# Weight-sum sets, operand splits and one low part at other places in a hand-scheduled retention and attention kernel

## The reference

```python
def retention_layer(x, w_in, w_out, pos):
    h = x @ w_in                                    # 1024 -> 6144
    q, k, v, g = jnp.split(h, [D_MODEL, 2 * D_MODEL, 2 * D_MODEL + RET_WIDTH], axis=-1)
    q = rope(q.reshape(bsz, s, RET_HEADS, RET_QK_DIM), pos)
    k = rope(k.reshape(bsz, s, RET_HEADS, RET_QK_DIM), pos) * RET_QK_DIM ** -0.5
...
    att = jnp.einsum('bhncd,bhnmd->bhncm', qc, kc) * dec[None, :, None]
    inner = jnp.einsum('bhncm,bhnme->bhnce', att, vc)
...
        cross = jnp.einsum('bhcd,bhde->bhce', qn, state) * xi
        state = state * g_chunk + jnp.einsum('bhcd,bhce->bhde', kn * zeta, vn)
...
    return (jax.nn.silu(g) * r) @ w_out             # 2048 -> 1024

def swa_layer(x, w_in, w_out, sinks, k_band, v_band, bias, key_valid):
    q, gate = jnp.split(x @ w_in, 2, axis=-1)
    sc = jnp.einsum('bncvgd,bnkvd->bvgnck', q, k_band) + bias
...
    m = jnp.maximum(sc.max(-1, keepdims=True), sink)
    p = jnp.exp(sc - m)
    p = p / (p.sum(-1, keepdims=True) + jnp.exp(sink - m))
    o = jnp.einsum('bvgnck,bnkvd->bncvgd', p, v_band)
    return (o * jax.nn.silu(gate)) @ w_out
```

## Time and profile before

| | |
|---|---|
| median of 3 runs | 2386.39 us |
| the three runs | 2385.63, 2386.39, 2390.29 us |
| the profiled execution | 2392.8 us |
| its span in the trace | 2391.0 us |
| PE busy | 2324.5 us, 97% |
| DVE busy | 1776.2 us, 74% |
| ACT busy | 1180.2 us, 49% |
| POOL busy | 329.6 us, 14% |
| DMA, mean over the span | 183 GB/s, 437.10 MB |

### The profile page before, as it was taken

The page is one execution under the profiler, slowest core; times in us unless marked ns, Lnnn a source line. Parts: engine busy times, 40 slices in busy tenths (PEclk is TensorE's granted clock), DMA queues, the critical chain, the costliest instruction groups (busy, mean ns, idle before and its releaser), DMA issues.

```text
span 2391.0 us, 31112 instructions
## 1 busy us (share of the span) xinstructions
PE 2324.5 (97%) x11554; PEld 1898.8 (79%) x11554; DVE 1776.2 (74%) x2575; ACT 1180.2 (49%) x1757; POOL 329.6 (14%) x346
## 2 busy tenths in 40 slices
PE   8999999999999999999999999999999999999996
PEld 6878878877788888887788888888777888888775
DVE  7778798856857669885696866886488668788458
ACT  4344455357435445535754545553665445453463
POOL 1212211112000111111201001110110110011032
PEclk9999999999999999999999999999999999999998
DMA  8776668643725445864384454575257344454323
GB/s 306 260 274 244 232 220 295 227 160 119 260 96 164 153 128 172 288 223 155 118 286 132 164 167 132 172 269 177 71 174 261 128 132 159 132 199 145 117 79 123
DMA packets 211798, 437.10 MB, mean 183 GB/s; under 512 B 14848, under 2 KB 52240, under 8 KB 208064
## 3 DMA queue, kind: packets, MB, share of 16 engines
q1 hardware_dynamic: 197568, 369.28, 46.6%
q0 software_dynamic: 14080, 65.83, 7.6%
HBM read 373.45 MB, written 57.41 MB: 180 GB/s over the span
## 4 chain that ended last, share of the span: by engine, by line
PE 76%; DVE 11%; DMA 5%; issue 4%; ACT 2%; SPq 1%; POOL 0%; DVEq 0%; ACTq 0%; POOLq 0%
PE accs L693 21%; PE accs L694 20%; PE accs L695 20%; DVE w_lo L1396 3%; PE bank L693 3%; PE bank L695 3%; PE bank L694 3%; DMA stage<-t_prep 2%; PE bank L959 2%; DMA stage<-ret_w_in 2%; PE bank L968 1%; PE bank L978 1%; PE bank L799 1%; ACT w_hi L1044 1%; DVE z L1721 1%
## 5 line engine op out<-in xcount | busy, mean ns | idle before, releaser
L1396 DVE TENSOR_TENSOR w_lo<-stage,w_hi 128x1024 fp32r<-128x1024 f32 x524 | 650.7, 1248 | 372.8 <-ACT w_hi L1044 371.3
L1044 ACT ACTIVATE w_hi<-stage 128x1024 fp32r<-128x1024 f32 x524 | 550.8, 1056 | 499.7 <-PE accs L695 184.7
L693 PE MATMUL accs<-w_hi,xs 128*128 128x512 f32 x1136 | 451.4, 397 | 12.2 <-DVE w_lo L1396 4.8
L695 PE MATMUL accs<-w_hi,xs 128*128 128x512 f32 x1136 | 444.2, 391 | 0.0
L694 PE MATMUL accs<-w_lo,xs 128*128 128x512 f32 x1136 | 443.9, 391 | 0.0
L693 PEld LDWEIGHTS accs<-w_hi,xs 128*128 128x128 f32 x1136 | 214.4, 189 | 61.1 <-issue 10.8
L695 PEld LDWEIGHTS accs<-w_hi,xs 128*128 128x128 f32 x1136 | 214.1, 188 | 45.8
L693 PE MATMUL accs<-x_hi,w_hi 128*128 128x512 f32 (+1 forms) x640 | 247.4, 387 | 2.7 <-DVE qT L1958 1.4
L694 PEld LDWEIGHTS accs<-w_lo,xs 128*128 128x128 f32 x1136 | 214.6, 189 | 42.5
L694 PE MATMUL accs<-x_lo,w_hi 128*128 128x512 f32 (+1 forms) x640 | 238.8, 373 | 0.0
L695 PE MATMUL accs<-x_hi,w_lo 128*128 128x512 f32 (+1 forms) x640 | 237.1, 371 | 0.0
(11 more groups left out here) (205 smaller groups left out, 3805.3 us busy)
## 6 DMA issues: line engine op xcount, KB each, us to landing
stage<-t_prep SPq DMA_DIRECT2D x208, 512.0 KB, 4.4
stage<-ret_w_in SPq DMA_DIRECT2D x100, 512.0 KB, 3.9
stage<-ret_w_in SPq DMA_DIRECT2D x128, 256.0 KB, 2.9
stage<-swa_w_in SPq DMA_DIRECT2D x64, 512.0 KB, 4.1
t_prep<-t_buf POOLq DMA_DIRECT2D x28, 1024.0 KB, 5.9
stage<-ret_w_out SPq DMA_DIRECT2D x48, 512.0 KB, 3.7
cs<-rope_t SPq DMA_DIRECT2D x16, 1024.0 KB, 7.1
t_buf<-ret_w_in POOLq DMA_DIRECT2D x32, 512.0 KB, 9.1
```

The costliest lines, as they stand in the source:

```text
L693: mm(dst, lhs[0], rhs[0], start=start, stop=False, skip_group_check=reopened)
L695: return mm(dst, lhs[1], rhs[0], start=False, stop=stop, skip_group_check=reopened)
L1044: copy(w_hi[:, RING[g] % HS], stage[:, RING[g] % LS], ACT.Copy).then_inc(w_hi_made, 1)
L1396: nc.vector.tensor_tensor(w_lo[:, RING[g] % LS], stage[:, RING[g] % LS], w_hi[:, RING[g] % HS].bitcast(F32), sub).then_inc(w_split, 1)
```

## The change

Five edits, four of them to tables of slots.

- Set 16 is loaded in slot 30 of block 0 (it was 23).
- Set 23 is loaded, made and stored one slot earlier.
- Sets 25, 26, 27 of block 0 and 1, 2, 3 of block 1 are made in slots 108, 110, 112 (they were made in 104, 106, 109). Their loads stay.
- Parts 1 and 2 of the readout operand are split in slots 65 and 67 (they were split in 63 and 65), in all four blocks, on ACT and DVE.
- In slot 8 of blocks 0 and 1 (plain heads) DVE makes the two halves of `v_lo` first and `qr_lo` behind them. In other heads the order stays.

```diff
-          (14, 2, 0, 22, 31, 31), (15, 1, 0, 25, 34, 34), (16, 3, 0, 23, 36, 36), (17, 2, 0, 35, 38, 38),
+          (14, 2, 0, 22, 31, 31), (15, 1, 0, 25, 34, 34), (16, 3, 0, 30, 36, 36), (17, 2, 0, 35, 38, 38),
...
-          (0, 0, 1, 88, 100, 100), (1, 2, 1, 100, 104, 104), (2, 3, 1, 100, 106, 106), (3, 4, 1, 103, 109, 109)]
+          (0, 0, 1, 88, 100, 100), (1, 2, 1, 100, 108, 108), (2, 3, 1, 100, 110, 110), (3, 4, 1, 103, 112, 112)]
...
-RO_SPLITS = {61: 0, 63: 1, 65: 2, 76: 3, 78: 4, 80: 5, 81: 6, 82: 7, 85: 8, 86: 9, 87: 10, 89: 11, 90: 12, 92: 13}
+RO_SPLITS = {61: 0, 65: 1, 67: 2, 76: 3, 78: 4, 80: 5, 81: 6, 82: 7, 85: 8, 86: 9, 87: 10, 89: 11, 90: 12, 92: 13}
...
+            def split_query(H):
+
+                dve.wait_ge(q_hi_made, H + 1)
+                nc.vector.tensor_tensor(qr_lo[:], qrT[:], qr_hi[:].bitcast(F32), sub).then_inc(q_split, 1)
...
+                        if v == 4 and not plain_head(H):
+                            split_query(H)
                         if v == 4:
-                            dve.wait_ge(q_hi_made, H + 1)
-                            nc.vector.tensor_tensor(qr_lo[:], qrT[:], qr_hi[:].bitcast(F32), sub).then_inc(q_split, 1)
                             dve.wait_ge(v_hi_made, 2 * H + 1)
                         if plain_head(H) and v == 4:
                             nc.vector.tensor_tensor(v_lo[:, 0:2, :], accs[:, 0:2, :], v_hi[:, 0:2, :].bitcast(F32),
...
                             nc.vector.tensor_tensor(v_lo[:, 2:4, :], accs[:, 2:4, :], v_hi[:, 2:4, :].bitcast(F32),
                                                     sub).then_inc(y_free, 2)
+                            split_query(H)
                             make_lo(ahead(g))
```

## The result

The changed kernel took 2369.87 us (median of 4 runs, 2366.7 to 2371.96). In the same comparison the kernel before took 2388.34 us. The ratio is 0.992, with a 95% interval of 0.9904 to 0.9936: 15 to 23 us faster, in the middle 19. The forecast was 22.6 us faster and 2363.8 us, with a range of 2357 to 2375. The direction and the range held; the gain was 3 to 4 us smaller than forecast, and the parts did not contribute as forecast. One execution in the later comparison of set 23 took 12086.23 us, and its ratio leaves it out.

The account below looks back on a forecast made before the run. TensorE's matmul stream, busy 97%, was taken as the bound. Savings of 3.3 + 2.9 + 4.1 + 5.0 + 7.3 = 22.6 us took the median from 2386.39 to 2363.8 us, range 2357 to 2375.

Parts of the forecast that it names:

- the chain of part 4: Block 0, x sum's store through moves of k and v to PE's attention start: 14.0 us, 11.05 without sets.
- part 4: Three late sets moved to slots 108 to 112 in blocks 0 and 1: saves 5.0 and 7.3 us.
- Block 1's term: Waits of 1.40 (qT) and 3.66 (moves), less 0.5 left over, plus 2.7 of half clock: 7.3 us saved.
- The leftover wait: What stays of PE's wait for the moves of k and v: 0.5 us taken per block.
- Part 3: Operand parts split at slots 65 and 67, set 23 a slot earlier: 4.1 us saved, from 1.5 to 5.9.
- The 1.8: Block 0: DVE's 0.66 idle at 348.92 filled, PE's stops of 0.60 and 0.52 at 364.39 and 365.56 gone.
- Part 2: Set 16 loaded at slot 30 instead of 23, block 0: 2.9 us saved, from 0 to 5.2.
- the case that the first stop stays and the second goes: Gain too late for the stop at 142.36, only the one at 151.62 goes: 1.9 us instead of 2.9.
- Part 1: Slot 8, blocks 0 and 1, v_lo ahead of qr_lo: 3.3 us saved, from 0.5 to 4.2.
- the half-clock stretch at 60.70: Block 0, behind slot 8's stop: assumed to go when 0.9 us of the stop is left, saving 1.7.
- Rival 1: The clock does not come back: 6.1 us missing, 16.5 saved, 2369.9 us; chance 0.17.

Follow-up runs that it names:

- before_again: The kernel before, unchanged, profiled a second time in one execution: 2386.37 us.
- set16_only: The kernel before with only set 16 loaded in slot 30 instead of 23: 2389.1 us against 2389.62, ratio 0.9992.
- set23_only: The kernel before with only set 23 one slot earlier: 2387.56 us against 2387.42, ratio 0.9999.
- splits_only: The kernel before with only operand parts 1 and 2 split in slots 65 and 67: 2386.21 us against 2389.62, ratio 0.999.
- vlo_only: The kernel before with only both halves of v_lo ahead of qr_lo in the plain heads: 2389.05 us against 2389.62, ratio 0.9992.
- late_only: The kernel before with only the six late sets moved to slots 108, 110, 112: 2378.14 us against 2389.62, ratio 0.9952.
- bias_later: The changed kernel with POOL's bias_rep transfer in slot 50 instead of 30: 2373.48 us, ratio to before 0.9944.
- bias_set20: The changed kernel with the bias transfer in slot 50 and set 20 loaded and made one slot earlier: 2370.18 us, ratio to before 0.9923.
- sets_doubled: The changed kernel with four more DVE instructions in each of the six late sets and set 0: 2378.54 us, ratio to before 0.9958.
- kv_first_before: The kernel before with the moves of k and v ahead of the x sum's store in SP's queue: 2383.45 us against 2387.49, ratio 0.9984.

## Why the prediction was right, and where it was off

The main cause was named rightly: the sets between the x sums delayed the moves of k and v, and in the softmax's slots they are covered. It was not the whole of it: the sets also held DVE's own way into the softmax, which the chain of part 4 left out. The parts alone, with set 23, add up to 17.9 us against 19 for the whole. The sizes, part by part:

**Part 4, forecast 12.3, measured 11.5 (7.6 to 15.3) alone.** For the sizes by block, six profiles have the old places of the sets and of the moves: 52.84, 52.25, 50.78, 52.55, 53.61 and 52.40 for slots 106 to 113 of block 0, mean 52.4; 55.12, 52.88, 51.53, 51.67, 53.83 and 53.28 for block 1, mean 53.1. Against 47.15 that is 5.3 (forecast 5.0) and 5.9, or 4.3 with the changed kernel's 48.76 (forecast 7.3). Block 1's term was over-sized because the profiled execution was the worst of the six there, and ran 5.4 us of work at half clock behind the stop; in three others (before_again, set16_only, set23_only) that stretch is half as long, in two (splits_only, vlo_only) there is none. The leftover wait, taken as 0.5 in each block, was 0 and 1.54 in the changed kernel's profile, and 0 in both blocks of late_only, bias_later, bias_set20 and sets_doubled. Taking the sets' cost in the new place as 0 was right: the window has the length of block 2's.

**Part 3, forecast 4.1, alone 2.4 (0 to 4.8) and 0.2 for set 23.** Blocks 1 to 3 gained somewhat more than forecast: slots 60 to 66 of the changed kernel take 21.02 us each, against 22.04 to 22.10 in the kernel before, 3.1 us together instead of 2.3. Block 0 was forecast to give back what it gains and to save 1.8 elsewhere. The giving back happened: over four profiles with the new splits (those with the bias transfer at slot 30) slots 60 to 66 take 20.1 on average, over seven with the old ones 22.5, and slots 66 to 84 take 68.7 against 66.8, so 0.5 is left. The 1.8 failed. The stops at slots 77 and 78 are 0.83 and 0.52 in the changed kernel, not gone. The row had named the right releaser: rT starts when the store lands, at 361.15 in the kernel before (issued at 354.71, landed 6.4 later), at 358.22 in set23_only (350.71, 7.5) and at 358.63 in the changed kernel:

```profile
349.69 0.63 POOL L2059 DMA_DIRECT2D t_prep<-t_buf  x1 [3.03 <-DVE t_buf L1460]
...
358.63 1.09 ACT L1147 ACTIVATE rT<-bank 128x512 f32<-128x512 f32 x2 [5.43 <-DMA t_prep<-t_buf]
```

The step that failed is that a store issued earlier lands earlier. Counted from PE's start behind the stop for state (358.57 before, 355.81 in the changed kernel) it was issued 6.12 us ahead instead of 3.86, 2.3 earlier, but it took 8.9 us instead of 6.4, and rT starts 2.8 behind that point instead of 2.6. Where it did land earlier, in set23_only, the stop for state had grown by 0.8. That stop is DVE's: it is busy for all of the stretch, and its load sets when state is ready.

**Part 2, forecast 2.9, measured 1.9 with an interval that holds 0.** Four profiles with set 16 at slot 30 take 51.46, 53.15, 52.54 and 52.62 us for slots 24 to 36, mean 52.4; seven with it at 23 take 52.87 to 55.23, mean 54.1. That is 1.7 us of the 2.9. The stops of the stretch, all added up, are 4.98 to 5.97 in the four and 4.63 to 8.21 in the seven, at changing places; that the one of slot 28 would take the gain is not borne out, since set16_only has 3.36 a slot earlier. Why less than the 2.9 us of transfer time came back the runs don't show. That DMA is what this stretch hangs on they do: without the bias transfer it takes 48.12, 50.07 and 48.44. Of the rule of the Trainium skill ("DMA: Bandwidth & Descriptors", section "Queues, rings and completion order") the prediction had made the case that the first stop stays and the second goes; in the changed kernel's profile the first is 0.78 and the second 3.15, but so it is, nearly, in two profiles with set 16 at 23, and the length of this stretch differs by 2.4 us where the code in it is the same: no run here tells the order of packets.

**Part 1, forecast 3.3, measured 1.9 with an interval that holds 0.** The stops shrank as forecast, by 0.9 and 0.5. The step that failed is the assumption that the half-clock stretch at 60.70 goes with the stop: it was not there in five of seven profiles of the old order. Slots 24 to 36 hang on DMA, and how much of block 0's 0.9 survives them the runs can't resolve.

So the forecast's 22.6 had 1.7 (part 1) and 2.7 (part 4, block 1) of clock in it that most other executions had in part or not at all, and 1.8 for block 0 of part 3, of which 0.5 came. In the other direction it left out three half-clock stretches of the kernel before (142.60, 152.90, 313.30), the second chain of part 4 and 0.8 of blocks 1 to 3. That the sum still came out near is partly such errors against each other. The profiled execution was 6.4 us above the median, and the prediction noted that and carried the whole saving over all the same; the profiled pair differs by 20.8. That is, as far as the profiles tell it, the main source of the difference between 22.6 and 19. Rival 1 (16.5) was half true: some stretches went with their stops, others came and went without them.

## What to carry to other kernels

When a profiled execution is several us above the median, some of its stops or its slow-clock stretches are its own, and a saving summed from them has to be shrunk; a second profile of the same kernel would have shown it. The same holds behind the change: a stop that shrank in one pair of profiles may be short in other executions of the old code too. A transfer issued earlier need not land earlier: look at what else is in transfer at its new place. A transfer's wait is best looked for in the queue of the engine that issues it and one step further back: here 3.7 us of waiting for a transfer began with four instructions of 2.9 us together on another engine. And where one engine is busy for all of a stretch, as DVE in slots 65 to 76 of block 0, removing a stop in front only moves it behind; where it is idle, as in the softmax, 2.9 us of work cost nothing and 4.7 do.

## What the runs showed of the hardware

The length of a stop alone did not decide whether the granted clock fell to 0.50, the 1.2 GHz level, behind it. At slot 8 it fell behind stops of 1.98 us (before) and 2.19 (late_only), and stayed at 1.00 behind 2.17 at the same matmul in before_again, set16_only and kv_first_before. At slot 108 windows of 3.3 us right behind the stop show 0.50 to 0.59 for stops of 3.82, 3.66, 3.54, 3.51, 3.44, 3.39, 3.10, 2.78 and 2.52 (before, set16_only, vlo_only, set23_only, before_again), and 1.00 for 3.23, 2.88 and 2.79 (splits_only, vlo_only), and for 1.54 in the changed kernel.

The same 1 MB store, issued at the same place of the code, took 5.3 us to land in the changed kernel and 8.0 in bias_later (set 20); set 23's took 6.4 in the kernel before and 8.9 in the changed kernel, one slot earlier.

Slots 24 to 36 of block 0, with the DMA engines busy to 0.76 in the kernel before, took 52.87 to 55.23 us in seven profiles with the same sets there; slots 106 to 113 of block 2, at 0.52, took 47.15 to 47.16 in every profile.
